# GLA half chunks laid between the MLA blocks, rotated keys on 128 rows, and softmax normalised by a diagonal matmul

## The chip, the cores and the metric

The kernel runs on one core of one Trainium2 chip. The metric is the time of one execution on the device in microseconds; several runs are compared by their median. TensorE is called PE, VectorE DVE, ScalarE ACT, GpSimd POOL, and SyncE SP; PEld is PE's loading of weights (the stationary operand). A matmul whose operands fill r partitions is said to use r rows of PE. PE's clock has two levels here, 1.2 GHz (a granted clock of 0.50) and 2.4 GHz (1.00).

## The reference, cut to what matters

The program is one inference step of a two-layer encoder on 272 prompt tokens (16 of them learned) and 32 sample tokens. Layer 0 starts with a mixer of two parallel parts, and only this stage is touched:

```python
# GLA, 4 heads (dk 64, dv 128), chunks of 64 tokens, state s of each head carried along
o_inter = einsum('bhtd,bhdv->bhtv', qc * exp(b), s)
att = einsum('bhtd,bhsd,bhtsd->bhts', qc, kc, decay)
o = o_inter + einsum('bhts,bhsv->bhtv', att, vc)
s = exp(b_last)[..., None] * s + einsum('bhsd,bhsv->bhdv', kc * exp(b_last - b), vc)
...
o_gla = rms_norm(o_gla, gla_norm_g) * silu(r)
# MLA, 8 heads over shared latent keys (128) and rotated keys (32)
s = (einsum('bhqc,bkc->bhqk', ql, k_lat) + einsum('bhqr,bkr->bhqk', qr, k_rope)) * MLA_SCALE
p = softmax(where(k_chunk <= q_chunk, s, NEG_INF))
o_lat = einsum('bhqk,bkc->bhqc', p, k_lat)
...
out = concatenate([o_gla, o_mla]) @ w_out0
```

The rest (layer norms, a routed MoE with 64 experts in each layer, a pooling mixer in layer 1) is the same in both kernels.

## The kernel before

All tokens lie in three tiles (`TILES`) of 128, 128 and 64 rows; the last holds 16 prompt tokens and the 32 sample tokens. There are six GLA chunks, `CHUNKS`: 0 to 3 are 64 tokens of the prompt, 4 its last 16, and 5 the sample, with a state of its own (`s_s`; the prompt's is `s_p`). All matrices are float32.

The order of the work on each engine is that of the code, written out by hand. PSUM is eight banks that `bank_uses` deals out in turn, by a list of named uses; use n of the list can't start before use n - 8 has been emptied (`banks.open`), `banks.full` waits for the fill and `banks.copied` for the emptying of a use. The uses of this stage, and who empties them:

- `att(t, h)`: level products of GLA, seven per chunk, K and M of 64 (L1005). DVE masks and sums them (`sum_levels`, L1621 and L1625) into `att`.
- `ql(h)`: absorbed queries, 64 rows, 320 columns (L1032); ACT copies them to `q_lat`. `qrT(i)`: `q_rot` transposed (24 transposes, L749); ACT copies them to `q_rot_t`.
- `o(c, j)` and `u(c, j)`, for each chunk c and pair of heads j: output of the chunk (L1018, the state against `qe_t` on 128 rows, and L1022, `att` against `v` on 64 rows or fewer) and update of the state (L1025). ACT copies `o` to `og`; `update_state` on DVE (L1637) adds `u` to the state, which the next chunk needs.
- `s(i)`, `pt(i)`, `ol(i)` for the 19 attention blocks: block 2h has head h's first 128 queries and 144 keys, block 2h + 1 the next 128 and 272 keys; block 16 packs the last prompt queries of all heads (272 keys), 17 and 18 the sample's (320 keys). `s` is two matmuls in one sum, `kv_t` on 128 rows and `kr_t` on 32. `scores` on DVE adds the mask and takes the maximum (L1670, L1672, L1493), ACT takes exp with its sum (L1375), DVE the reciprocal (L1684) and the product with it (L1493). PE transposes the probabilities (`pt`, L749: two tiles for 144 keys, three for 272 or 320, the last of 16 or 64 keys), ACT copies them to `p_t`, PE multiplies them with `ckv_n` or `past` (`ol`, L765, one matmul per key tile, the last on 16 or 64 rows), and DVE copies that back into `q_lat` (`latent_out`, L1497). A float32 matmul shows as two instructions in the trace, a transpose as one.

The block loop on PE issues for each i: s(i), pt(i - 2), ol(i - 3). DVE does for each m: reciprocal and product of m, `scores(m + 2)`, `latent_out(m - 2)`. All level products and chunks stand ahead of the loop, tile by tile. Between them and the blocks the squares of `og` are summed (`gss`), ACT makes `grs` of them with two changes of its table, and `norm_out` scales `og` after blocks 1, 3 and 5. After the loop come the transposes of `og` (`ogT`, waiting for `og_ready`), `om`, and the output projection `mo` (starts at 249.28 us). POOL sends the GLA states out when the last `u` is done, and SP waits for `og_ready` before it loads the router and the shared expert.

## Time and profile before

| | |
|---|---|
| median of 3 runs | 1508.03 us (1506.62 to 1508.96) |
| the profiled execution | 1507.37 us, span 1505.6 us |
| PE busy | 1435.9 us, 95% of the span |
| DVE, ACT, POOL busy | 634.3, 348.5, 49.1 us |
| mean granted clock of PE | 0.942 |
| this stage, level products to the start of `mo` | 102 to 249.3 us |

Busy time is what the engine's own instructions cover; where matmuls overlap or load weights in between, PE counts as busy all the time. The granted clock is the share of 2.4 GHz in a stretch; a stretch that spans a change shows a value between 0.50 and 1.00.

### The profile page before, as it was taken

Reading aid. Unit: us, or ns where it says so; the run is one execution under the profiler, and the core shown is the slowest. Engines: PE = TensorE matmul, PEld = TensorE weight load, DVE = VectorE, ACT = ScalarE, POOL = GpSimd, SP = SyncE. Lnnn points to the kernel's source line nnn. Section 1 sums busy time; section 2 is a strip of 40 time slices with the busy share of each in tenths; the row PEclk is TensorE's granted clock in tenths of the full one; section 3 lists DMA queues with packets and bytes.
Section 4 is the critical chain, followed back from the end, with each engine's and each line's share of the span. In section 5 each row is a group of like instructions: output and inputs, shape, how many; then the busy total and the mean of one; then the engine's idle time right before and its main releaser. Section 6 shows DMA issues by size and latency. Waiting matters only on the chain.

```text
span 1505.6 us, 17800 instructions
## 1 busy us (share of the span) xinstructions
PE 1435.9 (95%) x6519; PEld 753.0 (50%) x6519; DVE 634.3 (42%) x1267; ACT 348.5 (23%) x722; POOL 49.1 (3%) x77
## 2 busy tenths in 40 slices
PE   6999899899999999999999978999999999999994
PEld 4565465464454454455445465545445445444542
DVE  0554542562433343344334368334334333433436
ACT  1441321221221222122122213122212122222211
POOL 5200100100000000000000020000000000000000
PEclk9996557899999999999999989999999999999997
DMA  9102020176998999899899842599989989998970
GB/s 297 62 6 113 8 91 0 65 300 270 375 391 349 410 387 393 366 394 392 347 412 391 349 151 103 205 372 391 390 364 395 392 348 410 390 390 364 395 305 31
DMA packets 63623, 435.21 MB, mean 289 GB/s; under 512 B 4324, under 2 KB 6436, under 8 KB 13537
## 3 DMA queue, kind: packets, MB, share of 16 engines
q1 hardware_dynamic: 60800, 427.08, 71.0%
q0 software_dynamic: 2784, 7.62, 1.6%
q8 instruction: 24, 0.39, 0.1%
q14 instruction: 15, 0.12, 0.0%
HBM read 432.93 MB, written 1.76 MB: 289 GB/s over the span
## 4 chain that ended last, share of the span: by engine, by line
PE 93%; DVE 4%; issue 1%; ACT 1%; DMA 0%; SPq 0%; DVEq 0%
PE bank L849 30%; PE bank L765 25%; PE bank L797 15%; PE bank L791 12%; PE bank L749 4%; PE bank L859 1%; PE bank L919 1%; DVE sb_x L1519 1%; PE bank L1025 1%; PE bank L906 1%; DVE sb_x L1515 1%; PE bank L1022 1%; DVE sb_ln_st L1511 1%; PE bank L1018 1%; DMA sb_x<-in_x_sample_dram 0%
## 5 line engine op out<-in xcount | busy, mean ns | idle before, releaser
L1448 DVE TENSOR_TENSOR sb_x<-sb_x,bank 128x512 f32<-128x512 f32 (+1 forms) x396 | 242.0, 678 | 118.7 <-PE bank L791 118.7
L797 PE MATMUL bank<-sb_wslot,sb_ht 128*64 128x512 f32 x1024 | 231.0, 593 | 0.0
L849 PE MATMUL bank<-sb_wslot,sb_xg_own 128*64 128x512 f32 x1024 | 226.5, 595 | 1.7 <-ACT sb_xg_own L1216 1.7
L849 PE MATMUL bank<-sb_wslot,sb_xt 128*64 128x512 f32 x1024 | 226.8, 595 | 0.0
L1467 DVE TENSOR_TENSOR sb_hh<-sb_sg,bank 128x256 f32<-128x256 f32 x64 | 27.0, 421 | 376.8 <-ACT sb_sg L1240 376.8
L1454 DVE SCALAR_TENSOR_TENSOR sb_yl<-bank,sb_gslot,sb_yh 128x512 fp32r<-128x512 f32 x128 | 96.0, 750 | 162.8 <-ACT sb_yh L1222 162.8
L765 PE MATMUL bank<-sb_pick,sb_xh 128*128 128x512 f32 x432 | 160.8, 401 | 0.9 <-DVE sb_x L1817 0.9
L791 PE MATMUL bank<-sb_yh,sb_place 128*128 128x512 f32 x396 | 157.6, 398 | 3.3 <-DVE sb_yl L1454 3.3
L791 PE MATMUL bank<-sb_yl,sb_place 128*128 128x512 f32 x396 | 156.6, 395 | 0.0
L1240 ACT ACTIVATE sb_sg<-bank 128x256 f32<-128x256 f32 x64 | 24.6, 384 | 550.1 <-PE bank L849 550.1
L797 PEld LDWEIGHTS bank<-sb_wslot,sb_ht 128*64 128x64 f32 x1024 | 72.8, 137 | 144.6 <-issue 139.3
L849 PEld LDWEIGHTS bank<-sb_wslot,sb_xg_own 128*64 128x64 f32 x1024 | 71.4, 137 | 140.6 <-issue 139.6
L849 PEld LDWEIGHTS bank<-sb_wslot,sb_xt 128*64 128x64 f32 x1024 | 70.7, 137 | 139.5 <-issue 139.5
L1222 ACT ACTIVATE sb_yh<-bank,sb_gslot 128x512 fp32r<-128x512 f32 x128 | 88.1, 688 | 174.2 <-PE bank L797 174.2
L765 PE MATMUL bank<-sb_pick,sb_xl 128*128 128x512 f32 x288 | 113.7, 395 | 0.0
L765 PEld LDWEIGHTS bank<-sb_pick,sb_xh 128*128 128x128 f32 x432 | 81.3, 188 | 19.1 <-issue 2.6
L791 PEld LDWEIGHTS bank<-sb_yh,sb_place 128*128 128x128 f32 x396 | 74.3, 188 | 27.3 <-DVE sb_x L1448 5.7
L791 PEld LDWEIGHTS bank<-sb_yl,sb_place 128*128 128x128 f32 x396 | 74.5, 188 | 17.1
L1216 ACT ACTIVATE sb_xg_own<-bank 128x512 f32<-128x512 f32 x80 | 47.9, 598 | 79.1 <-PE bank L765 79.1
L765 PEld LDWEIGHTS bank<-sb_pick,sb_xl 128*128 128x128 f32 x288 | 54.3, 188 | 10.1
L1216 ACT ACTIVATE sb_xt<-bank 128x512 f32<-128x512 f32 x64 | 38.3, 599 | 37.7 <-PE bank L765 37.7
L749 PEld LDWEIGHTS bank<-sb_cst,sb_hh 128*128 128x128 f32 x128 | 20.7, 205 | 46.0 <-issue 45.4
(297 smaller groups left out, 1201.1 us busy)
## 6 DMA issues: line engine op xcount, KB each, us to landing
sb_wslot<-in_moe_w_gate_dram SPq DMA_DIRECT2D x64, 2048.0 KB, 8.4
sb_wslot<-in_moe_w_up_dram SPq DMA_DIRECT2D x64, 2048.0 KB, 13.1
sb_wslot<-in_moe_w_down_dram SPq DMA_DIRECT2D x64, 2048.0 KB, 15.3
sb_w_in_hi<-in_w_in_dram SPq DMA_DIRECT2D x2, 2048.0 KB, 24.2
sb_w_in_lo<-in_w_out_dram SPq DMA_DIRECT2D x1, 4096.0 KB, 13.5
sb_w_in_lo<-in_w_in_dram SPq DMA_DIRECT2D x2, 1024.0 KB, 10.3
sb_ln_g<-in_ln_g_dram POOLq DMA_DIRECT2D x4, 512.0 KB, 4.5
sb_ln_b<-in_ln_b_dram POOLq DMA_DIRECT2D x4, 512.0 KB, 6.0
```

Source lines behind the costliest of these rows:

```text
L749: return pe.transpose(dst, src, ident[0:n, 0:n])
L765: last = pe.matmul(dst, lhs, rhs, start=i == 0, stop=i == len(pairs) - 1)
L791: last = pe.matmul(banks.tile[order[f]][:, :], place[u][:, t * P:(t + 1) * P], part[:, c * 512:(c + 1) * 512], start=h == 0, stop=h == 1)
L797: last = pe.matmul(y_b[c][64 * e:64 * e + 64, :], ht[:, k, 64 * e:64 * e + 64], w_down[u][:, e, k * D + c * 512:k * D + (c + 1) * 512], st ...
L849: last = pe.matmul(gu_b[64 * e:64 * e + 64, :], xgt[b][:, k, sl], w_gu[u][:, :, e, k * FE:(k + 1) * FE], start=k == 0, stop=k == DK_SLICES ...
L859: last = pe.matmul(place_b[:, t * PLACED:(t + 1) * PLACED], pick[b][:, t, q * P:(q + 1) * P], spread[:, b, t, :], start=True, stop=True)
L1216: act.activation(xgt[b][:, kk, :], banks.tile[2 + c][:, :], ACT.Copy).then_inc(s[f"xg_copied{c}"], 1)
L1222: act.activation(yh[:, c * 512:(c + 1) * 512], banks.tile[4 + c][:, :], ACT.Copy, scale=gslot[:, u, :]).then_inc(s[f"yh_ready{c}"], 1)
L1240: act.activation(sg[:, :], gu_b[:, 0:FE], ACT.Silu).then_inc(s["sg_ready"], 1)
L1448: dve.tensor_tensor(dst, dst, banks.tile[order[f]][0:rows, :], ALU.add).then_inc(s["added"], 1)
L1454: dve.scalar_tensor_tensor(out=yl[:, cc], in0=banks.tile[4 + c][:, :], scalar=gslot[:, u, :], in1=yh[:, cc].bitcast(F32), op0=ALU.mult, op ...
L1467: dve.tensor_tensor(hh[:, :], sg[:, :], gu_b[:, FE:2 * FE], ALU.mult).then_inc(s["h_ready"], 1)
```

## The change

It has three parts.

1. `CHUNK_PARTS` splits the six chunks into twelve half chunks (c, j), and one of them stands behind each of the first twelve iterations of the block loop: on PE `chunk_out(c, j)`, on ACT the copy of `o`, on DVE `update_state(c, j)` behind `latent_out`. All level products, `ql` and `qrT` come ahead of the loop. The squares of a tile are summed behind iterations 6, 10 and 13 of DVE's loop, `grs` is made in iteration 15 of ACT's, and `norm_out` stands in iterations 16, 17 and 18.
2. `kr_t` and `skr_t` get 128 rows, of which 32 to 127 are zero (one more memset on POOL), and `kr_t`'s matmul in `s` runs on 128 rows.
3. DVE doesn't multiply the probabilities by the reciprocal any more. POOL multiplies the identity by it (`diag`, 128x128, two buffers, the second use waits for `pt(m - 2)`), and `pt` becomes a float32 matmul of the raw exponentials against `diag`, which transposes and normalises.

POOL's 19 `diag` instructions stand ahead of its stores of the GLA states.

```diff
+CHUNK_PARTS = [(c, j) for c in range(len(CHUNKS)) for j in range(2)]
+SQUARES_AT = (6, 10, 13)
+ROOT_AT, NORM_AT = 15, (16, 17, 18)
@@ bank_uses
-    for t in range(TILES):
-        u += [("att", t, h) for h in range(GH)]
...
+    u += [("att", t, h) for t in range(2) for h in range(GH)] + [("ql", h) for h in range(MH)]
+    u += [("att", 2, h) for h in range(GH)] + [("qrT", i) for i in range(5)]
     n = len(attention_blocks())
     for i in range(n + 3):
         u += [("s", i)] if i < n else []
         u += [("pt", i - 2)] if 0 <= i - 2 < n else []
         u += [("ol", i - 3)] if 0 <= i - 3 < n else []
+        u += [("o",) + CHUNK_PARTS[i], ("u",) + CHUNK_PARTS[i]] if i < len(CHUNK_PARTS) else []
@@ gpsimd
+            gp.memset(kr_t[:, :], 0.0).then_inc(zeroed, 1)
...
+            for m in range(len(attention_blocks())):
+                gp.wait_ge(inv_ready, m + 1)
+                if m >= 2:
+                    banks.full(gp, ("pt", m - 2))
+                gp.tensor_scalar(diag[:, m % 2, :], const("ident"), stat[:, m % 4, 3:4], None, ALU.mult).then_inc(diag_ready, 1)
@@ tensor engine
-                    ql, qr = q_lat[:, hs[0], q0:q0 + nq], q_rot_t[0:ROPE, hs[0], q0:q0 + nq]
+                    ql, qr = q_lat[:, hs[0], q0:q0 + nq], q_rot_t[:, hs[0], q0:q0 + nq]
...
-                    pe.wait_ge(p_ready, m + 1)
+                    pe.wait_ge(diag_ready, m + 1)
                     ps = banks.open(pe, ("pt", m))
                     for k, rows in key_tiles(m):
-                        last = transpose(pe, ps[0:rows, k * P:(k + 1) * P], sm[:, m % 4, k * P:k * P + rows])
+                        last = pe.matmul(ps[0:rows, k * P:(k + 1) * P], sm[:, m % 4, k * P:k * P + rows], diag[:, m % 2, :],
+                                         start=True, stop=True)
...
+                if i < len(CHUNK_PARTS):
+                    chunk_out(*CHUNK_PARTS[i])
@@ scalar engine, block loop
+                if m < len(CHUNK_PARTS):
+                    c, j = CHUNK_PARTS[m]
+                    tc, pb, n = CHUNKS[c]
+                    copy(og[pb:pb + n, tc, j * 256:(j + 1) * 256], ("o", c, j), lambda ps: ps[pb:pb + n, 0:256])
+                if m == ROOT_AT:
+                    act.wait_ge(gss_ready, TILES)
+                    rsqrt(grs[:, :], gss[:, :], 1.0 / GDV, eps[:, 1:2], grs_ready)
@@ vector engine, block loop
                 dve.wait_ge(ex_ready, m + 1)
-                step(dve.reciprocal(stat[:, m % 4, 3:4], stat[:, m % 4, 2:3]))
-                ts(sm[:, m % 4, 0:nk], sm[:, m % 4, 0:nk], stat[:, m % 4, 3:4], None, ALU.mult, None, p_ready)
+                dve.reciprocal(stat[:, m % 4, 3:4], stat[:, m % 4, 2:3]).then_inc(inv_ready, 1)
                 if m + 2 < len(blocks):
                     scores(m + 2)
                 if m >= 2:
                     latent_out(m - 2)
-                if m == 0:
+                if m < len(CHUNK_PARTS):
+                    update_state(*CHUNK_PARTS[m])
+                if m in SQUARES_AT:
+                    square_sums(SQUARES_AT.index(m))
+                if m == NORM_AT[0]:
                     dve.wait_ge(grs_ready, 1)
-                if m in (1, 3, 5):
-                    norm_out(m // 2)
+                if m in NORM_AT:
+                    norm_out(NORM_AT.index(m))
```

On PE, an odd slot of the block loop before: s with 272 keys, a pt of three tiles, an ol of two. `waits` names semaphores: emptied2 says that bank 2 is free, p_ready that the probabilities are normalised; `sb_w_in_hi` is the memory that `q_lat`, `q_rot_t`, `sm` and `p_t` share, and sizes are those of output rows and columns.

```order
L765 MATMUL bank0<-sb_kv_t,sb_w_in_hi 128x272 [waits emptied0]
L765 MATMUL bank0<-sb_kr_t,sb_w_in_hi 128x272
L749 MATMUL bank1<-sb_cst,sb_w_in_hi 128x128 [waits emptied1,p_ready]
L749 MATMUL bank1<-sb_cst,sb_w_in_hi 128x128
L749 MATMUL bank1<-sb_cst,sb_w_in_hi 16x128
L765 MATMUL bank2<-sb_w_in_hi,sb_ckv_n 128x128 [waits emptied2,emptied6]
L765 MATMUL bank2<-sb_w_in_hi,sb_ckv_n 128x128
```

The same slot (i = 5) now:

```order
L770 MATMUL bank4<-sb_kv_t,sb_w_in_hi 128x272 [waits emptied4]
L770 MATMUL bank4<-sb_kr_t,sb_w_in_hi 128x272
L1082 MATMUL bank5<-sb_diag,sb_w_in_hi 128x128 [waits emptied5,diag_ready]
L1082 MATMUL bank5<-sb_diag,sb_w_in_hi 128x128
L1082 MATMUL bank5<-sb_diag,sb_w_in_hi 16x128
L770 MATMUL bank6<-sb_w_in_hi,sb_ckv_n 128x128 [waits emptied6,emptied0]
L770 MATMUL bank6<-sb_w_in_hi,sb_ckv_n 128x128
L1021 MATMUL bank7<-sb_s_p,sb_qe_t 64x256 [waits emptied7,emptied6]
L1025 MATMUL bank7<-sb_v,sb_att 64x128 [waits att_ready] x2
L1028 MATMUL bank0<-sb_v,sb_kd 128x256 [waits emptied0]
```

Behind ol there now stand the output and the update of a half chunk. The bank of ol, bank 6, was that of the `u` of two slots before, and the chunk's first matmul waits for the same emptying (emptied6).

On DVE, one iteration of the block loop before, from a product of the probabilities on (`filled` says that PE has filled a bank):

```order
L1493 TENSOR_SCALAR sb_w_in_hi<-sb_w_in_hi,sb_stat 128x144 [waits dve_step]
L1670 SCALAR_TENSOR_TENSOR sb_w_in_hi<-bank5,sb_mix 128x144 [waits filled5,filled0,p_ready]
L1672 TENSOR_REDUCE sb_stat<-sb_w_in_hi 128x1 [waits emptied5]
L1493 TENSOR_SCALAR sb_stat<-sb_stat 128x1 [waits dve_step]
L1497 COPY sb_w_in_hi<-bank4 128x128 [waits filled4,mx_ready]
```

The iteration that belongs to the slot shown for PE, now:

```order
L1683 RECIPROCAL sb_stat<-sb_stat 128x1 [waits ex_ready,emptied1]
L1670 SCALAR_TENSOR_TENSOR sb_w_in_hi<-bank4,sb_mix 128x272 [waits filled4,filled3]
L1672 TENSOR_REDUCE sb_stat<-sb_w_in_hi 128x1 [waits emptied4]
L1496 TENSOR_SCALAR sb_stat<-sb_stat 128x1 [waits dve_step]
L1500 COPY sb_w_in_hi<-bank1 128x128 [waits filled1,mx_ready]
L1639 SCALAR_TENSOR_TENSOR sb_s_p<-sb_s_p,sb_u_t,bank6 64x128 [waits filled6]
L1639 SCALAR_TENSOR_TENSOR sb_s_p<-sb_s_p,sb_u_t,bank6 64x128 [waits dve_step]
```

The product is gone, and two instructions that add `u` of bank 6 to the state are now behind scores of bank 4 and the copy of bank 1.

## Rows read from the trace of the kernel before

**Rows 1.** The page, parts 1 and 2: busy time; granted clock in 40 slices.
```profile
PE 1435.9 (95%) x6519; PEld 753.0 (50%) x6519; DVE 634.3 (42%) x1267; ACT 348.5 (23%) x722; POOL 49.1 (3%) x77
...
PEclk9996557899999999999999989999999999999997
```

**Rows 2.** Windows: length, busy us (instructions) by engine, granted clock, DMA share, GB/s.
```profile
107.50:111.20 3.70, 2.20 (x7) 0.87 (x8) 3.09 (x4) 1.33 (x4) 0.00 (x0) 1.00 0.00 0
...
116.50:121.50 5.00, 5.00 (x113) 4.96 (x112) 3.72 (x6) 0.00 (x0) 0.00 (x0) 0.50 0.02 3
121.50:124.85 3.35, 3.35 (x20) 2.23 (x16) 3.15 (x5) 1.67 (x3) 0.00 (x0) 0.50 0.00 0
...
131.00:135.10 4.10, 2.40 (x11) 0.83 (x10) 3.71 (x12) 0.38 (x1) 0.00 (x0) 1.00 0.81 277
135.10:159.40 24.30, 20.95 (x52) 8.75 (x52) 6.10 (x18) 3.93 (x12) 0.00 (x0) 0.50 0.31 126
...
171.80:241.80 70.00, 70.00 (x200) 44.01 (x199) 29.82 (x103) 17.29 (x67) 0.00 (x0) 0.50 0.12 49
```

**Rows 3.** Timeline of PE, 121 to 250 us: start, us, instructions.
```profile
121.58 4.05 PE L749 MATMUL bank<-sb_cst,sb_q_rot 128*32 128x128 f32 x24
...
249.28 1.10 PE L765 MATMUL bank<-sb_w_in_lo,sb_xt 128*128 128x512 f32 x2 [0.94 <-DVE sb_xt L1497]
```

**Rows 4.** Timeline of PE, two slots of the attention blocks.
```profile
188.12 0.85 PE L765 MATMUL bank<-sb_kv_t,sb_w_in_hi 128*128 128x144 f32 x2
188.90 0.84 PE L765 MATMUL bank<-sb_kr_t,sb_w_in_hi 32*128 32x144 f32 x2
...
191.87 1.27 PE L765 MATMUL bank<-sb_kv_t,sb_w_in_hi 128*128 128x272 f32 x2
193.07 1.27 PE L765 MATMUL bank<-sb_kr_t,sb_w_in_hi 32*128 32x272 f32 x2
194.28 0.90 PE L749 MATMUL bank<-sb_cst,sb_w_in_hi 128*128 128x128 f32 x3
194.97 1.36 PE L765 MATMUL bank<-sb_w_in_hi,sb_ckv_n 128*128 128x128 f32 x4
196.26 0.61 PE L765 MATMUL bank<-sb_kv_t,sb_w_in_hi 128*128 128x144 f32 x1
```

**Rows 5.** Timeline of PE, half chunks at both clocks.
```profile
125.55 0.65 PE L1018 MATMUL bank<-sb_s_p,sb_qe_t 128*64 128x256 f32 x2
...
127.33 0.65 PE L1018 MATMUL bank<-sb_s_p,sb_qe_t 128*64 128x256 f32 x2
...
137.60 1.11 PE L1018 MATMUL bank<-sb_s_p,sb_qe_t 128*64 128x256 f32 x2
...
140.84 1.11 PE L1018 MATMUL bank<-sb_s_p,sb_qe_t 128*64 128x256 f32 x2
```

**Rows 6.** Timeline of DVE, state updates and two blocks.
```profile
137.78 0.73 DVE L1637 SCALAR_TENSOR_TENSOR sb_s_s<-sb_s_s,sb_u_t,bank 64x128 f32<-64x128 f32 x2 [1.18 <-PE bank L1025]
...
189.88 0.31 DVE L1670 SCALAR_TENSOR_TENSOR sb_w_in_hi<-bank,sb_mix 128x144 f32<-128x144 f32 x1 [0.28 <-PE bank L765]
...
190.75 0.29 DVE L1497 COPY sb_w_in_hi<-bank 128x128 f32<-128x128 f32 x1
...
194.48 0.44 DVE L1670 SCALAR_TENSOR_TENSOR sb_w_in_hi<-bank,sb_mix 128x272 f32<-128x272 f32 x1 [2.98 <-PE bank L765]
...
195.62 0.29 DVE L1497 COPY sb_w_in_hi<-bank 128x128 f32<-128x128 f32 x1
```

**Rows 7.** Groups of POOL: busy us, mean ns.
```profile
L720 POOL TENSOR_TENSOR sb_wslot<-sb_wslot 128x1024 f32<-128x1024 f32 x2 | 4.7, 2336 | 571.6 <-DMA sb_wslot<-in_pool_scale_dram 571.6
```

**Rows 8.** Timeline: level sums on DVE, a table load on ACT.
```profile
104.28 0.62 DVE L1621 TENSOR_TENSOR sb_att_m<-bank,sb_mix 128x448 f32<-128x448 f32 x1
...
105.89 0.62 DVE L1621 TENSOR_TENSOR sb_att_m<-bank,sb_mix 128x448 f32<-128x448 f32 x1
...
159.22 1.28 ACT L1269 ACT_TABLE_LOAD   x1
```

More of the change, by code:

```diff
@@ L62 @@
 SLOTS = 64
-ZEROED = 2 + 9 + 2
+ZEROED = 2 + 9 + 3
 MIX_PARAMS = 11
@@ L400, in build @@
         stat = mb("stat", [P, 4, 4])
+        diag = mb("diag", [P, 2, P])
         mixer_ctx.close()
@@ L1323, in _ @@
                 act.activation(kv_t[:, cols], ps[:, 256:256 + rows], ACT.Copy)
-                act.activation(kr_t[:, cols], ps[0:ROPE, 384:384 + rows], ACT.Copy).then_inc(banks.empty_sem(n), 1)
+                act.activation(kr_t[0:ROPE, cols], ps[0:ROPE, 384:384 + rows], ACT.Copy).then_inc(banks.empty_sem(n), 1)
             for g in range(TILES):
@@ L1626, in sum_levels, with update_state @@
                              att_ready if i + 1 == len(parts_) else None)
-            def update_state(c):
+            def update_state(c, j):
                 t, pb, n = CHUNKS[c]
                 st = s_s if c == 5 else s_p
-                for j in range(2):
-                    name = ("u", c, j)
-                    ps = banks.full(dve, name)
-                    last = t * P + pb + n - 1
-                    for b in range(2):
-                        hp, hc = slice(64 * b, 64 * b + 64), slice(128 * b, 128 * b + 128)
-                        ins = dve.scalar_tensor_tensor(out=st[hp, j, hc], in0=st[hp, j, hc], scalar=u_t[hp, j, last:last + 1],
-                                                       in1=ps[hp, hc], op0=ALU.mult, op1=ALU.add)
-                        step.banked(ins, banks, name) if b else step(ins)
+                name = ("u", c, j)
+                ps = banks.full(dve, name)
+                last = t * P + pb + n - 1
+                for b in range(2):
+                    hp, hc = slice(64 * b, 64 * b + 64), slice(128 * b, 128 * b + 128)
+                    ins = dve.scalar_tensor_tensor(out=st[hp, j, hc], in0=st[hp, j, hc], scalar=u_t[hp, j, last:last + 1],
+                                                   in1=ps[hp, hc], op0=ALU.mult, op1=ALU.add)
+                    step.banked(ins, banks, name) if b else step(ins)
             dve.wait_ge(state_in, 16 * GH)
@@ L1643, in _, with square_sums @@
                 sum_levels(t)
-                for c in CHUNKS_BY_TILE[t]:
-                    update_state(c)
-            for c in range(len(CHUNKS)):
-                for j in range(2):
+            def square_sums(t):
+                rows = ROWS[t]
+                for c, j in CHUNK_PARTS[4 * t:4 * t + 4]:
                     banks.copied(dve, ("o", c, j))
-            for t in range(TILES):
-                rows = ROWS[t]
                 tt(sq[0:rows, :], og[0:rows, t, :], og[0:rows, t, :], ALU.mult)
```

85 lines of the change are left out of this document (33 added, 52 removed).

## The prediction

> **What bounds the kernel now.** I read the page first. PE is busy 95% of the span [rows 1], so time can only come from shorter or faster work on PE or from its gaps. The change touches one stage, so next I cut that stage with the windows view [rows 2]. From the level products (102 us) to the output projection (249.3 us [rows 3]) PE runs at two speeds: the granted clock is 1.00 (2.4 GHz) to 111.2, 0.50 (1.2 GHz) to 124.85, 1.00 to 135.1, and 0.50 from there to about 248 (the clock row of the page has a 7 in its seventh slice, 225.8 to 263.5) [rows 1, 2]. PE is busy 70.00 of 70.00 us in the attention blocks and still has half its clock. Nothing waits for DVE there: DVE works 29.8 us and ACT 17.3 us of the 70. So the 112 us at 0.50 are the prize, and the number of PE cycles is the second item.
>
> What did PE do before the clock moved? [rows 2, 3] It rose at 124.85 after transposes of q_rot, all with 128 rows and without gaps, since 121.58 us. It did not rise after five full microseconds of level products on 64 rows (116.5 to 121.5), nor in 24 us of GLA chunks, nor in 70 us of blocks, where kr_t occupies 32 rows, the last key tile 16, and 128-row work comes in shorter pieces [rows 4]. It fell at 111.2 and 135.1 after stretches in which PE was busy 2.20 of 3.70 us and 2.40 of 4.10 us, with 64 rows and fewer. Rows used and gaps are what differs; I take that as the mechanism.
>
> The Trainium skill ("TensorE: Matmul & The Clock Gate", Part 4: PE-mode transpose) says that transposes do not bring the full clock, as they don't count as PE-busy in the same way. This trace disagrees: the rise at 124.85 follows transposes alone. By that rule matmuls in the place of the blocks' transposes would bring the full clock and the time of the case "full throughout" below.
>
> By the row, transposes are as good as any 128-row work for the clock, so I credit their replacement with nothing.
>
> **The change, part by part, in PE time at 0.50.** A *slot* is what PE does for one i of the block loop: s, pt, ol and, new, a half chunk. Before, an even slot (144 keys) takes 188.12 to 191.87 = 3.75 us and an odd one (272 keys) 191.87 to 196.25 = 4.38 [rows 4], 8.13 a pair.
> - *pt as matmul*: kv_t takes 0.78 us for 144 columns and 1.20 for 272, so 128 columns stream in 0.42 us. A transposed tile takes (194.97 - 194.28)/3 = 0.23 [rows 4]. Five tiles a pair: +5 x 0.2 = +1.0 us.
> - *kr on 128 rows*: kr_t costs as much as kv_t (0.78, 1.20), so more rows cost nothing. Of each 0.78, 144 x 0.42/128 = 0.47 streams and 0.31 does not; four matmuls of the ol tiles take 1.29 us from 194.97 for 0.85 of streaming, so part of this time goes where the number of rows stays the same. If kr and the first pt tile lose it: -0.3 to -0.5 a slot; nothing and -0.6 are the bounds. With the line above: 8.0 to 9.1 us a pair, and I take 8.2.
> - *Half chunks moved*: one takes 137.60 to 140.84 = 3.24 us at 0.50, and 125.55 to 127.33 = 1.78 at 1.00 [rows 5]. Twelve move, none vanishes. PE's idle time around them, 3.35 us of 135.1 to 159.4 alone [rows 2], goes.
> - *DVE*: 19 normalisations of the probabilities go, each shorter than a scores instruction of the same columns (0.31, 0.44) [rows 6]. POOL gets 19 tensor_scalar of 128x128. The trace has none; the nearest row is a two-input product of 128x1024 at 2.34 us, which is 0.29 for 128 columns and the other bound whole [rows 7]. I take 0.45, near the end with the same columns. It lies under s and pt of later slots as long as chunks stand between them; in the tail at the full clock each 0.5 us more would cost up to 4.
> - *kr_t memset*: one more at the start, where POOL waits for w_in next. The state stores now stand behind 19 diag instructions on POOL and the shared loads of SP behind a late og_ready; both are needed only after mo. Nothing.
>
> **The new wait.** This is what the order decides. DVE runs scores(i), latent_out(i-4), update_state(i-2) in that order, and scores(i) waits for s(i). On PE, ol(i-3) of slot i opens the bank that u(i-2) used (eight banks in turn, five uses a slot), and chunk i needs the state of i-2. So in slots 4 to 12 PE does s(i), pt(i-2), then stands until DVE is through: 0.2 us from the end of s to DVE (194.28 to 194.48), scores 1.14 (272 keys) or 0.87 (144), latent_out 0.33, two state updates 0.77 (0.29 and 0.73 and the steps between), 0.07 back [rows 4, 6]: 2.5 us in odd slots, 2.25 in even ones. Behind the standing ol(i-3) in PE's queue are the chunk and s(i+1), for which DVE waits in turn. pt covers 1.28 (three tiles) or 0.85 at 0.50, and half of that at 1.00.
>
> s at 0.50 is 1.20 + 1.21 - 0.3 = 2.1 us in odd slots and 0.78 + 0.78 - 0.3 = 1.25 in even ones; ol is 1.15 (the 1.29 above less what I count with the next s) and a tile more, 1.6.
>
> At 0.50: odd 2.1 (s) + 2.5 + 1.15 (ol) + 3.24 = 9.0; even 1.25 + 2.25 + 1.6 + 3.24 = 8.3. At 1.00: odd 1.07 + 2.5 + 0.58 + 1.78 = 5.95; even 0.63 + 2.25 + 0.79 + 1.78 = 5.45. Slots 0 to 3 have less to wait for, no wait in the first two and no latent_out in the next: 4.5 + 5.3 + 6.4 + 7.8 = 24.0 us at 0.50, 2.4 + 2.9 + 4.3 + 5.0 = 14.6 at 1.00. Slots 4 to 11: 8 x 8.65 = 69.2, or 8 x 5.7 = 45.6. So the chunk slots are 93.2 or 60.2 us.
>
> *Start.* DVE's level sums (104.28 to 105.89, 1.61 us a head [rows 8]) pace the absorbed queries, which reuse their banks: 104.28 + 8 x 1.61 = 117.2, then one ql, tile 2's levels (an estimate of 3.7 for both at 0.50), the rotations (4.05 [rows 3]), and ACT's last copies (an estimate of 1.6): slot 0 at 126.7.
>
> *Tail* (slots 12 to 21): 40.4 us of PE at 0.50 (four slots of 4.1 with 1.8 of the wait, then the 320-key blocks and the drain, 22 us now). At 1.00: 20.2 plus about 6.3 of waits, since reciprocals now queue behind square_sums and norm_out (an estimate of 1.4 us each) and exp behind grs with two table loads of 1.3 each [rows 8]: 26.5. From the last ol to mo: 241.8 to 249.28, 7.5 at 0.50 [rows 2, 3], 4.9 at 1.00.
>
> *Sums against the 249.28 at which mo starts in the profiled execution:*
> - clock full throughout: 126.7 + 60.2 + 26.5 + 4.9 = 218.3, or -31.
> - half in the chunk slots, full again early in the tail, where no chunk stands between runs of 128 rows (about 8 us at 0.50 first, then 32.4/2 and 5.3 of the waits, 29.5): 126.7 + 93.2 + 29.5 + 4.9 = 254, or +4 to +5.
> - half throughout: 126.7 + 93.2 + 40.4 + 7.5 = 267.8, or +18.5.
>
> With a share h of the chunk slots at 0.50 it is about -30 + 33h. The profiled execution is 1507.37 (span 1505.6) and the median 1508.03, 0.7 apart, so differences carry over.
>
> **Which h?** An odd slot at 0.50 now has s and pt unbroken on 128 rows, 2.1 + 1.3 = 3.4 us, like the 3.3 us of transposes after which the clock rose, but only once in 17 us, with a wait behind it. Each slot at 1.00 has 1.85 us of standing still, then a 16-row tile and 64-row products, much like what stood before both falls. So I expect it to rise at the rotations or in the first blocks, to fall again once or twice, and to be full in the tail. I choose h = 0.6: -9 to -10 us, **1499 us**. By case: h under 0.2 (1477 to 1485), 0.28; mixed (1485 to 1506), 0.42.
>
> **Rivals.**
> - *All full* (case one, 0.28): 1477, if a standing PE of 1.85 us a slot is too little to lower the clock. For: before both falls PE stood for 1.5 and 1.7 us and the rest had 64 rows and fewer, while here s, pt and half of the chunk have 128. Against: the 1.85 us in every slot.
> - *Half in the chunk slots* (0.20): 1508 to 1513. For: the chunks, which at 0.50 never raised the clock in 24 us, are laid between the runs of 128 rows. It decides from h = 0.9 up.
> - *Half throughout* (0.10): slower, +18.5, 1526. One mechanism: the ping-pong of PE and DVE adds about 1.3 us to eight slots and the tail's waits cut its runs too. It speaks against it that plain slots have over 3.4 us without a break.
> - *Transposes hold the clock down* (0.05, within the first case): as matmuls they would let s, pt and ol run as one piece that raises and keeps the clock, and the time is that of all full, 1477. Against: the row of the q_rot transposes ahead of the rise at 124.85.
> - *The wait isn't there* (within the first case): then chunk slots at 0.50 are 7.3 us and at 1.00 3.7; 1461 at full clock. Against: the order of DVE.
>
> **Chances.** A measurement tells about 0.2%, 3 us, from no change. Faster 0.68, same 0.12 (half of the third case and the edge of the mixed one), slower 0.20. The range reaches from all full to the third case: 1476 to 1514; the likeliest case's own is 1485 to 1506. The time left out is half throughout and the absent wait.
>
> **What would show it.** Right: slot 0 near 127; chunk slots of 5.5 or 8.7 us; PE waiting for update_state before ol or qe in each, 1.8 us at 1.00 and 1.3 at 0.50; no PE wait for diag in slots 2 to 11; clock changes inside the stage; time after mo unchanged. Wrong: the clock 0.50 to the end of the tail; diag instructions over 1 us with pt waiting for them; pairs of plain slots over 8.5 us at 0.50, if unhidden weight loads remain between kr and pt.

## The result and the profile after

The changed kernel takes 1515.3 us (median of 20 executions) against 1507.7 for the kernel before (20 beside them): a ratio of 1.0047, 95% interval 1.0037 to 1.0058. It is slower by 7 to 8 us; the forecast was 9 us faster. The profiled execution has a span of 1511.8 us, 6.2 more than before, and the output projection starts 6.15 us later (255.43 against 249.28 [rows 3]), so all of it lies ahead of the projection. Of all executions below, two stand far out and enter no ratio: one of e9_tail_only took 2085.7 us at a mean clock of 0.644, one of the kernel before 4939 us.

The page of the changed kernel, busy time and granted clock, against [rows 1]:

```profile
PE 1432.3 (95%) x6568; PEld 755.0 (50%) x6568; DVE 627.9 (42%) x1248; ACT 349.1 (23%) x723; POOL 61.5 (4%) x97
...
PEclk9996558999999999999999988999999999999997
```

The slices moved a little: 5 5 8 9 where 5 5 7 8 9 stood. So I cut the changed kernel's stage at the places where the clock moves (windows view; columns as in [rows 2]):

```profile
120.96:124.37 3.41, 1.47 (x16) 1.02 (x14) 2.45 (x8) 3.27 (x9) 0.00 (x0) 1.00 0.97 386
124.37:144.85 20.48, 19.31 (x52) 11.11 (x52) 5.20 (x18) 4.06 (x13) 1.21 (x2) 0.50 0.33 135
144.85:151.68 6.83, 5.32 (x29) 3.18 (x29) 2.09 (x9) 2.34 (x10) 1.21 (x2) 1.00 0.00 0
151.68:175.57 23.89, 21.26 (x61) 12.92 (x60) 5.66 (x20) 2.96 (x13) 1.21 (x2) 0.50 0.00 1
175.57:182.40 6.83, 5.00 (x27) 3.28 (x28) 3.19 (x10) 2.13 (x8) 0.60 (x1) 1.00 0.00 0
182.40:189.22 6.82, 6.51 (x18) 3.33 (x18) 1.83 (x7) 0.27 (x1) 0.60 (x1) 0.50 0.00 0
189.22:192.64 3.42, 2.79 (x14) 1.58 (x15) 0.61 (x3) 1.03 (x5) 0.60 (x1) 1.00 0.01 2
192.64:223.36 30.72, 27.61 (x85) 17.51 (x84) 10.31 (x35) 5.55 (x23) 3.02 (x5) 0.50 0.00 1
223.36:240.42 17.06, 12.98 (x67) 8.90 (x66) 10.13 (x28) 7.42 (x20) 3.45 (x5) 1.00 0.00 0
240.42:254.08 13.66, 13.66 (x51) 9.26 (x52) 5.11 (x11) 2.56 (x6) 4.32 (x9) 0.50 0.71 268
```

The clock now rises four times in the blocks, and each time it is lost again. In each stretch at 1.00 PE is idle for part of the time (busy 5.32 of 6.83, 5.00 of 6.83, 2.79 of 3.42, 12.98 of 17.06). The waits view of PE, 124 to 256 us (us in total, times, longest), names what it stands for:

```profile
PE bank L770 <- DVE sb_s_p L1639: 8.9, 8, 1.5
PE bank L1082 <- POOL sb_diag L711: 4.1, 2, 2.6
...
PE bank L770 <- DVE sb_s_s L1639: 1.1, 1, 1.1
PE bank L1021 <- DVE sb_s_p L1639: 1.0, 1, 1.0
```

L1639 is update_state, 11.0 us in ten waits; L711 is GpSimd's diagonal. PE's timeline, an even slot begun at 1.00 and the odd one after it at 0.50:

```profile
147.20 0.51 PE L770 MATMUL bank<-sb_kv_t,sb_w_in_hi 128*128 128x144 f32 x2
147.55 0.41 PE L770 MATMUL bank<-sb_kr_t,sb_w_in_hi 128*128 128x144 f32 x2
147.79 0.71 PE L1082 MATMUL bank<-sb_diag,sb_w_in_hi 128*128 128x128 f32 x4
150.01 1.10 PE L770 MATMUL bank<-sb_w_in_hi,sb_ckv_n 128*128 128x128 f32 x6 [1.51 <-DVE sb_s_p L1639]
...
153.78 1.27 PE L770 MATMUL bank<-sb_kv_t,sb_w_in_hi 128*128 128x272 f32 x2
...
155.75 1.60 PE L1082 MATMUL bank<-sb_diag,sb_w_in_hi 128*128 128x128 f32 x6
158.28 1.49 PE L770 MATMUL bank<-sb_w_in_hi,sb_ckv_n 128*128 128x128 f32 x4 [0.93 <-DVE sb_s_p L1639]
...
239.41 1.07 PE L1082 MATMUL bank<-sb_diag,sb_w_in_hi 128*128 128x128 f32 x6 [2.65 <-POOL sb_diag L711]
240.41 1.94 PE L770 MATMUL bank<-sb_w_in_hi,sb_ckv_n 128*128 128x128 f32 x6
```

The wait is where the prediction put it and a little shorter than it said (1.51 for 1.8 at 1.00, 0.93 to 1.09 for 1.2 to 1.4 at 0.50). Two of the three falls in the chunk slots, at 151.68 and 182.40, come 1.7 and 1.1 us after such a wait. But the slots at 0.50 have the wait too, and two of the rises (175.57 and 189.22) fell inside one, so this trace alone does not show that the wait lowers the clock; the experiments ask that. The last two rows are the tail: PE stands 2.65 us for the diagonal of block 17, and 1 us later the clock falls and stays down for 13.66 us. DVE's timeline shows why that diagonal is late:

```profile
236.49 0.68 DVE L1493 TENSOR_TENSOR sb_og<-sb_og,sb_grs 128x512 f32<-128x512 f32 x1
237.20 0.69 DVE L1493 TENSOR_TENSOR sb_og<-sb_og,sb_g_gla 128x512 f32<-128x512 f32 x1
237.93 0.16 DVE L1683 RECIPROCAL sb_stat<-sb_stat 128x1 f32<-128x1 f32 x1
```

The reciprocal stands behind a whole norm_out, which stands behind the scores of block 18. The diagonal then took 1.17 us (from 238.19) beside the next norm_out, where the other 18 took 0.60 or 0.61 us. The groups of POOL give the price of a diagonal, the unknown of the prediction (busy us, mean ns):

```profile
L711 POOL TENSOR_SCALAR sb_diag<-sb_cst,sb_stat 128x128 f32<-128x128 f32 x19 | 12.1, 634 | 151.8 <-DVE sb_stat L1683 151.8
```

**The balance.** The same cut of the kernel before, windows view:

```profile
111.19:124.85 13.66, 13.66 (x142) 9.77 (x142) 7.56 (x12) 2.42 (x5) 0.00 (x0) 0.50 0.01 1
124.85:135.09 10.24, 8.54 (x126) 4.51 (x124) 5.94 (x19) 2.36 (x6) 0.00 (x0) 1.00 0.33 112
135.09:247.73 112.64, 107.09 (x301) 62.16 (x303) 48.39 (x149) 26.95 (x93) 4.20 (x8) 0.50 0.15 60
```

From 111 us to the projection, count PE's busy time at 0.50 once and at 1.00 twice: that is its work in microseconds at 0.50. Before, 120.8 us busy at 0.50 and 9.2 at 1.00 (0.6 of them after 247.73) make 139.1, and PE is idle 8.2 of 138.1 us. Now 98.1 (9.7 of them before 120.96) and 28.0 make 154.1, and it is idle 18.6 of 144.7. So work grew by 15.0 and idle time by 10.4, and 18.8 more busy microseconds at the full clock gave back 18.8: +6.6, by which this stretch is longer. Three questions follow: what lifts the clock, what lowers it, and which part made PE's work 15 us more.

### The profile page after: what moved, and what is told of

Its sections match the earlier page's. It is cut to its first block, busy times and chain, and to the rows that moved or that the text cites. A ratio compares the mean times of both kernels' runs of the same rounds, so it can differ in the third digit from the quotient of the medians.

```text
span 1511.8 us, 17919 instructions
## 1 busy us (share of the span) xinstructions
PE 1432.3 (95%) x6568; PEld 755.0 (50%) x6568; DVE 627.9 (42%) x1248; ACT 349.1 (23%) x723; POOL 61.5 (4%) x97
## 4 chain that ended last, share of the span: by engine, by line
PE 91%; DVE 5%; issue 2%; ACT 1%; DMA 1%; SPq 0%; POOL 0%; DVEq 0%; ACTq 0%; POOLq 0%
PE bank L854 30%; PE bank L770 24%; PE bank L802 15%; PE bank L796 12%; PE bank L754 3%; PE bank L864 1%; PE bank L924 1%; PE bank L1028 1%; PE bank L1025 1%; PE bank L911 1%; PE bank L1021 1%; DVE sb_x L1522 1%; DVE sb_ln_st L1514 1%; DVE sb_x L1518 1%; DMA sb_x<-in_x_sample_dram 1%
```

## Experiments

The changed kernel has three parts: half chunks between the blocks (part 1), the rotated keys and queries on 128 rows (part 2), and transposing by a matmul with the diagonal (part 3). Each run below was timed 5 to 12 times beside the kernel before; ratios are to that, with the 95% interval. The theories that the expectations name are: A, rows used and gaps set the clock; T, transposes hold it down; S, the keys on 32 rows hold it down; I, laying chunks between blocks lifts it; W, a standing PE lowers it; R, the 64-row and 16-row products lower it whatever PE waits for.

**Which part lifts the clock?** The first two runs split part 1 from the other two: `e1_parts_2_3` is the kernel before with parts 2 and 3, `e2_part_1` the changed kernel without them.

```diff
 # e1_parts_2_3, against the kernel before
-        kr_t = mb("kr_t", [ROPE, T_COLS])
+        kr_t = mb("kr_t", [P, T_COLS])
...
-                        last = transpose(pe, ps[0:rows, k * P:(k + 1) * P], sm[:, m % 4, k * P:k * P + rows])
+                        last = pe.matmul(ps[0:rows, k * P:(k + 1) * P], sm[:, m % 4, k * P:k * P + rows], diag[:, m % 2, :],
+                                         start=True, stop=True)
 # e2_part_1, against the changed kernel: both of these the other way round
```

> The kernel before with the diagonal and the keys on 128 rows, but the chunks where they stood: all six ahead of the blocks. The blocks follow one another with nothing of 64 rows between them, only the 16-row key tiles. Theory A (rows and gaps set the clock; transposes are as good as other 128-row work): a pair of blocks at 0.50 costs about what it did (8.1 us before, 8.2 by my sum), and since s, pt and ol had the same share of full rows before, the clock stays at 0.50 for most of the stage: -3 to +3 us against before. Rival T (transposes held the clock down; the Trainium skill, TensorE: Matmul & The Clock Gate, Part 4, says that they do not count as the matmuls do): with them gone the clock rises in the first blocks and the 86 us of blocks at 0.50 become about 50: -30 us or more. Rival S (the rotated keys on 32 rows held it down) gives the same time; the trace alone does not part S from T here, kernels with one of the two do.

Measured: 1489.8 us, 0.9879 (0.9859 to 0.9899), -18 us. Theory A as I had it (-3 to +3) falls, as it gave the wider keys no weight in the blocks; which of T and S it is, e5 and e6 below say. The clock was at 1.00 in two stretches of the blocks, of 10.24 us and this one (windows view):

```profile
190.20:220.92 30.72, 29.88 (x158) 21.35 (x158) 13.77 (x53) 10.61 (x42) 8.34 (x15) 1.00 0.22 88
```

> The changed kernel with the half chunks between the blocks, but transposes, normalisation on DVE and 32-row keys as before. Theory A (rows and gaps): at least as slow as the changed kernel, since the slots hold less 128-row work and DVE has 0.8 us more to do per slot ahead of update_state: the granted clock at 0.50 in nearly all of 126 to 250 and +10 to +20 us against before. Rival T (transposes are what keeps the clock down, in the changed kernel it was lifted where they went): no rise at all in the chunk slots and the tail, and +18 or more. Rival I (interleaving is what lifted the clock, whatever the tiles are): rises as in the changed kernel, five of them between 120 and 250, and 0 to +8 us.

Measured: 1526.8 us, 1.0126 (1.0105 to 1.0146), +19. Part 1 alone never lifts the clock: rival I falls, and A and T both foresaw this. The windows view of this run, one row from the rotations to the end of the stage:

```profile
123.90:263.80 139.90, 123.64 (x327) 67.20 (x327) 48.11 (x151) 28.54 (x96) 4.20 (x8) 0.50 0.08 31
```

**Rows or transposes?** Parts 2 and 3 were then taken singly on the kernel before.

```diff
 # e5_kr_only, against the kernel before: part 2 alone
-                        ql, qr = q_lat[:, hs[0], q0:q0 + nq], q_rot_t[0:ROPE, hs[0], q0:q0 + nq]
+                        ql, qr = q_lat[:, hs[0], q0:q0 + nq], q_rot_t[:, hs[0], q0:q0 + nq]
 # e6_diag_only, against the kernel before: part 3 alone
-                    pe.wait_ge(p_ready, m + 1)
+                    pe.wait_ge(diag_ready, m + 1)
```

> The kernel before with the rotated keys and queries on 128 rows and nothing else; transposes, DVE's normalisation and the place of the chunks stay. The run with both edits and the old place of the chunks took 1489.8 against 1507.8 and its clock was at 1.00 in 40.9 of the 73 us from 158 to 231, so one of the two (or both together) lifts it. Rival T (the transposes held it down): the clock stays at 0.50 to the end of the blocks, and only the weight loads between kr and pt go, -3 to -7 us. Rival S (the 32 rows held it down): the clock rises in the blocks, -20 to -30 us. If both edits are needed: as T.

Measured: 1481.0 us, 0.9836 (0.9821 to 0.9851), -26. One edit, and a better kernel than the change.

> The kernel before with the transposes replaced by matmuls with the diagonal from GpSimd, and nothing else; the rotated keys stay on 32 rows. Rival T: the clock rises in the blocks, -10 to -20 us. Rival S: it stays at 0.50, each tile costs 0.2 us more, 45 tiles or about +9 us, and the first slots wait for the diagonal as they did in the run with both (7.0 us in all there): +5 to +12 us. If both edits are needed: as S.

Measured: 1528.5 us, 1.0143 (1.0122 to 1.0165), +22. The windows of e5, then of e6:

```profile
186.91:222.17 35.26, 31.15 (x181) 22.79 (x181) 24.93 (x83) 14.34 (x52) 0.00 (x0) 1.00 0.24 98
```

```profile
134.20:267.30 133.10, 127.64 (x350) 72.17 (x352) 41.48 (x129) 26.46 (x93) 15.61 (x27) 0.50 0.13 50
```

With transposes and 128-row keys the clock rises for good 27 us into the blocks and stays at 1.00 to the projection; with matmuls for transposes and 32-row keys it never moves. Rival T falls, and rival S stands. What about the 32 rows does it is not shown: the same edit also takes 0.36 us a slot off PE (below), so these runs do not part the number of rows from whatever PE does in that time around a 32-row matmul.

The Trainium skill's rule that transposes do not bring the full clock ("TensorE: Matmul & The Clock Gate", Part 4) would have it the other way round; these two runs disagree with it.

e6 also prices part 3. PE's timeline of e6, an odd slot and an even one, against [rows 4]:

```profile
198.14 1.27 PE L772 MATMUL bank<-sb_kv_t,sb_w_in_hi 128*128 128x272 f32 x2
199.35 1.27 PE L772 MATMUL bank<-sb_kr_t,sb_w_in_hi 32*128 32x272 f32 x2
200.55 1.76 PE L1087 MATMUL bank<-sb_diag,sb_w_in_hi 128*128 128x128 f32 x6
202.24 1.52 PE L772 MATMUL bank<-sb_w_in_hi,sb_ckv_n 128*128 128x128 f32 x4
...
208.38 1.27 PE L772 MATMUL bank<-sb_kv_t,sb_w_in_hi 128*128 128x272 f32 x2
```

A pair takes 208.38 - 198.14 = 10.24 us where it took 8.13: +2.1, not the +1.0 of the sum. Three tiles take 1.69 us (200.55 to 202.24) where three transposes took 0.69 (194.28 to 194.97), and two products of the ol tiles behind them 1.45 for 1.29. Part 2 alone takes a pair from 8.13 to 7.42 (175.27 to 183.11 in e5, less a wait of 0.42). The changed kernel, with both, has 4.14 + 4.95 = 9.1 (slots 12 and 13, less a wait of 1.09). For 9.5 pairs, 0.95 us each, that is 9 of the 15 us by which the balance's work grew; the rest I have not traced.

**Do PE's waits lower the clock?** Two versions of the changed kernel keep all three parts and move only DVE's work.

```diff
 # e3_update_first, against the changed kernel
                 dve.reciprocal(stat[:, m % 4, 3:4], stat[:, m % 4, 2:3]).then_inc(inv_ready, 1)
+                if m < len(CHUNK_PARTS):
+                    update_state(*CHUNK_PARTS[m])
                 if m + 2 < len(blocks):
                     scores(m + 2)
                 if m >= 2:
                     latent_out(m - 2)
-                if m < len(CHUNK_PARTS):
-                    update_state(*CHUNK_PARTS[m])
 # e4_dve_ahead, on top of that: no scores(1) ahead of the loop; SQUARES_AT = (6, 10, 12), ROOT_AT = 13,
 # NORM_AT = (15, 16, 17); square_sums and norm_out here too, and then
-                if m + 2 < len(blocks):
-                    scores(m + 2)
-                if m >= 2:
-                    latent_out(m - 2)
+                if m + 1 < len(blocks):
+                    scores(m + 1)
+                if m >= 3:
+                    latent_out(m - 3)
```

> The changed kernel with one line moved: DVE does update_state(i) ahead of scores(i+2), not behind it. This takes away the wait of PE's ol for DVE (10 times, 1.0 to 1.5 us each, 11.0 us in all). Theory W (the standing PE is what lowers the clock in the chunk slots): the clock is at 1.00 for most of slots 0 to 11, they last 12 x 4 = 48 us instead of 85, so the kernel takes about 1480. Rival R (the 64-row products and 16-row tiles lower it, wait or not): the clock changes as often as before, only the waits go, slots of 7.3 us at 0.50 and 4 at 1.00, 8 to 12 us less than the changed kernel, about 1504.

Measured: 1477.1 us, 0.9801 (0.9779 to 0.9824): 38 us less than the changed kernel for one statement moved, of which 11 are the waits themselves. Its windows and one slot of its timeline:

```profile
122.91:136.56 13.65, 13.21 (x35) 7.16 (x36) 4.07 (x15) 3.93 (x12) 1.21 (x2) 0.50 0.54 217
136.56:201.41 64.85, 60.28 (x314) 39.29 (x314) 33.68 (x111) 23.03 (x81) 11.13 (x18) 1.00 0.00 1
201.41:211.66 10.25, 10.25 (x41) 7.31 (x41) 3.88 (x8) 2.23 (x6) 3.87 (x8) 0.50 0.69 254
```

```profile
142.18 0.51 PE L770 MATMUL bank<-sb_kv_t,sb_w_in_hi 128*128 128x144 f32 x2
...
146.24 0.72 PE L770 MATMUL bank<-sb_kv_t,sb_w_in_hi 128*128 128x272 f32 x2
```

Slots of 4.1 us, no wait in them, and the clock at 1.00 for 64.85 us: theory W holds here and rival R falls, since the 64-row products and the 16-row tiles are all still there. The clock falls once, after the 2.65 us for the diagonal of block 17, as in the changed kernel; a wait of 1.07 us for a diagonal at 188.4, at 1.00, is followed by no fall.

> The changed kernel with DVE's loop laid out anew: reciprocal, update_state, square_sums or norm_out, and only then the scores of the next block (one block ahead instead of two), so that the reciprocals, and with them the diagonals, are never queued behind a scores instruction that waits for PE; rsqrt on ACT comes two blocks earlier. This takes away the waits for update_state (11.0 us) and those for the diagonal (1.44 and 2.65 us, after which the clock fell at 240.4). Theory W: the clock stays at 1.00 from the first slots to the output projection, chunk slots 48 us, tail 22: about 1470. Rival R: it changes as often as in the changed kernel; chunk slots as in the run with update_state alone moved, and the tail's waits of 4 us go: 1500 to 1503.

Measured: 1471.4 us, 0.9766 (0.9743 to 0.9789). Two waits of about 1 us remain for the last diagonals, and the fall at 200.6 comes between them, so the full clock to the projection, which theory W had, did not come.

**The waits gone and the rows given back.** e8_first_kr32 is e3 with the keys on 32 rows, e7_first_transposes e3 with transposes.

```diff
 # e7_first_transposes, against e3_update_first
-                dve.reciprocal(stat[:, m % 4, 3:4], stat[:, m % 4, 2:3]).then_inc(inv_ready, 1)
+                step(dve.reciprocal(stat[:, m % 4, 3:4], stat[:, m % 4, 2:3]))
+                ts(sm[:, m % 4, 0:nk], sm[:, m % 4, 0:nk], stat[:, m % 4, 3:4], None, ALU.mult, None, p_ready)
 # e8_first_kr32, against e3_update_first
-        kr_t = mb("kr_t", [P, T_COLS])
+        kr_t = mb("kr_t", [ROPE, T_COLS])
 ... (skr_t, q_few_rot and the rows of qr likewise)
```

> The same run (1477.1 us) with the rotated keys and queries back on 32 rows; diagonal and half chunks between the blocks stay. If the 32 rows count (rival S): clock at 0.50 for most of 123 to 240, 1500 to 1510. If they do not (T or W): clock at 1.00 as there, and only the weight loads between kr and pt come back, 0.15 to 0.25 us a slot at the full clock: 1480 to 1483.

Measured: 1527.7 us, 1.0156 (1.0133 to 1.0179), 51 us more than e3, more than either theory said. Its windows view:

```profile
124.75:268.05 143.30, 142.96 (x388) 78.75 (x390) 42.15 (x135) 27.58 (x95) 15.62 (x27) 0.50 0.10 38
```

PE is busy 142.96 of 143.30 us, with matmuls where transposes stood, and the clock does not rise once. A PE that hardly ever stands is not enough; with the keys on 32 rows the clock stays down.

> The run with update_state ahead of the scores (1477.1 us, clock at 1.00 from 136.6 to 201.4), but with the transposes and DVE's normalisation back; half chunks between the blocks and keys on 128 rows stay. Rival T: without matmuls in the place of the transposes the clock falls back to 0.50 for all of 123 to 240 and the run takes 1500 to 1515. Rival W (the waits alone made the difference between the changed kernel and that run): the clock is at 1.00 as there, and the cheaper tiles make it 1470 to 1478.

Measured: three executions took 1463 to 1471 us and three 1496 to 1499 (median of all 1483.4; mean clocks 0.968 to 0.975 and 0.945 to 0.948). The ratio of 0.9738 (0.971 to 0.9766) is that of the first kind alone. Neither theory said two kinds. The profiled execution is of the first, at 1.00 from 139.1 to 180.1 us.

**The tail alone.**

```diff
 # e9_tail_only, against the changed kernel
-SQUARES_AT = (6, 10, 13)
-ROOT_AT, NORM_AT = 15, (16, 17, 18)
+SQUARES_AT = (6, 10, 12)
+ROOT_AT, NORM_AT = 13, (16, 17, 18)
 # and from turn 12 on square_sums and norm_out stand between the reciprocal and scores(m + 2)
```

> The changed kernel (1515.3 us) with its tail alone laid out anew: the last square_sums and the norm_outs stand between the reciprocal and the scores, where DVE waits for PE, rsqrt comes two blocks earlier on ACT, and the last norm_out follows the last reciprocal. The wait for update_state in the chunk slots stays. Theory W as I have it: the standing of 1.44 and 2.65 us for the diagonal shrinks to 1 us each at most, the fall at 240.4 goes with it, and blocks, ogT and om run to their end at 1.00: -4 (a third of it waits, the rest 8 us of work at the full clock in place of half) to -8 us against the changed kernel, 1507 to 1511. Rival: the fall comes from what stands ahead of it, not from the length of these two waits: -1.5 to -3 us, 1512 to 1514.

Measured: 1506.8 us, 0.9986 (0.9974 to 0.9998) to the kernel before: 9 us less than the changed kernel. PE's timeline there has 0.90 us in the place of the 2.65:

```profile
239.32 1.07 PE L1082 MATMUL bank<-sb_diag,sb_w_in_hi 128*128 128x128 f32 x6 [0.90 <-POOL sb_diag L711]
...
242.38 2.18 PE L770 MATMUL bank<-sb_w_in_hi,sb_past 128*128 128x128 f32 x12
...
249.25 1.10 PE L770 MATMUL bank<-sb_w_in_lo,sb_xt 128*128 128x512 f32 x2 [0.96 <-DVE sb_xt L1500]
```

From slot 13 to the projection it takes 249.25 - 219.16 = 30.1 us, where the changed kernel took 255.43 - 214.72 = 40.7, and the clock stays at 1.00 from 222.94 on. Of these 10.6 us the profiled execution gives back 4.4, as it reaches slot 13 later, though nothing ahead of it was edited. The tail alone turns the change from slower into no difference.

**The best of it.** Part 2 and the moved DVE work stay, part 3 goes. e10_kr_ahead has the chunks ahead of the blocks, e11_ahead_transposes between them; e12_ahead_few also takes the four copies of the few queries out of the way of the first block.

```diff
 # e10_kr_ahead: e5_kr_only with DVE's loop as in e4; e11_ahead_transposes: e4 with the transposes of e7
 # e12_ahead_few, against e11 (PE)
-            pe.wait_ge(skeys_ready, 2)
+            pe.wait_ge(skeys_ready, 1)
...
+                    if i == 2 * MH:
+                        pe.wait_ge(skeys_ready, 2)
 # and on ACT the copies to q_few and q_few_rot stand in turn 0 of its loop
```

> The run with the keys on 128 rows alone (1481.0 us; chunks ahead of the blocks, transposes, normalisation on DVE), with DVE's loop one block ahead: reciprocal, normalisation and norm_out, then the scores. There PE waited for normalised probabilities 8 times, 7.7 us in all, the longest 3.9. If these waits keep the clock down in the first blocks (it rose for good at 186.9 only, 27 us into them), it rises 10 to 20 us earlier: 1468 to 1474. If not, only the waits after the first go: 1476 to 1479.

Measured: 1479.5 us, 0.9802 (0.9788 to 0.9816), 1.5 us less than e5 (5 by the two ratios). DVE's waits did not keep the clock down there. The windows view shows it at 0.50 for 27 us with PE busy for 26 of them, all on 128 rows but for the 16-row tiles, and then at 1.00 with the same work; why there and not before stays open.

```profile
168.81:196.12 27.31, 26.11 (x82) 19.38 (x82) 18.48 (x57) 8.64 (x35) 0.00 (x0) 0.50 0.32 126
196.12:217.00 20.88, 19.95 (x115) 15.62 (x114) 15.85 (x54) 9.23 (x39) 0.00 (x0) 1.00 0.00 1
```

> The run with DVE's loop one block ahead (1471.4 us: half chunks between the blocks, keys on 128 rows), with the transposes and DVE's normalisation in the place of GpSimd's diagonal. A pair of blocks at 0.50 took 10.24 us with matmuls and 8.13 with transposes, so about 1 us a pair at the full clock: -8 us, and DVE, with 0.5 us more a block, has room (it waits for PE 26.8 of 75 us): 1461 to 1465. Rival T in its last form (transposes make the clock less steady): 1475 to 1495 and a wide spread, as in the run of the update alone with transposes, which took 1463 to 1499.

Measured: again two kinds, 1458 to 1467 us (four) and 1492 to 1494 (four); the ratio of the first kind is 0.969 (0.9668 to 0.9713). The profiled execution is of the second kind, and PE is busy throughout in it at half its clock:

```profile
127.00:196.44 69.44, 69.44 (x197) 41.66 (x197) 27.27 (x87) 13.45 (x50) 0.00 (x0) 0.50 0.07 26
```

> The run with the loop one block ahead and transposes, with the four copies of the few queries on ACT moved from ahead of the first block into its first turn, and PE's wait for them ahead of the block that reads them. This takes away most of the 2.1 us in which PE stands ahead of the first block. Theory W: the clock then stays at 1.00 from the rotations on (it rose at 122.1 and fell at 125.5 just there), and the first three slots, 13 us at 0.50, take 7: -8 us against that run. Rival R (the level products on 64 rows ahead lower it whatever PE waits for): -1.5 to -2 us, the wait alone.

Measured: 1460.4 us, 0.9681 (0.9665 to 0.9696), all five of one kind (1458.8 to 1466.7). The fall at the first block is gone, with a wait of 0.98 us there instead of 2.1; windows and PE's timeline:

```profile
124.67:182.70 58.03, 53.52 (x282) 34.66 (x281) 39.77 (x127) 26.09 (x86) 4.21 (x8) 1.00 0.18 69
```

```profile
181.33 1.12 PE L763 MATMUL bank<-sb_w_in_hi,sb_ckv_n 128*128 128x128 f32 x6 [2.59 <-ACT sb_w_in_hi L1384]
...
194.23 0.90 PE L747 MATMUL bank<-sb_cst,sb_w_in_hi 128*128 128x128 f32 x3 [2.57 <-DVE sb_w_in_hi L1491]
```

The clock falls 1.4 us after the first wait of 2.6 us (182.70) and during the second (192.94).

**Two questions left by these.** Do transposes count for less, which would explain the two kinds? e13_twice does each of e11's twice. Do the falls in e12's tail go with its waits? e14_few_tail moves rsqrt and norm_out.

```diff
 # e13_twice, against e11_ahead_transposes
-                        last = transpose(pe, ps[0:rows, k * P:(k + 1) * P], sm[:, m % 4, k * P:k * P + rows])
+                        for again in range(2):
+                            last = transpose(pe, ps[0:rows, k * P:(k + 1) * P], sm[:, m % 4, k * P:k * P + rows])
 # e14_few_tail, against e12_ahead_few (and rsqrt behind the copies of pt, not ahead)
-ROOT_AT, NORM_AT = 13, (15, 16, 17)
+ROOT_AT, NORM_AT = 12, (14, 15, 18)
```

> The run with the loop one block ahead and transposes (11 above: its clock stayed at 0.50 through the chunk slots in 4 of 8 executions, 1492 to 1494 us, and rose early in the others, 1458 to 1467), with every transpose of the probabilities done twice into the same place. The second ones do nothing but occupy 128 rows: a slot at 0.50 then has 3.9 us on 128 rows instead of 3.4, about what the matmuls with the diagonal gave, beside the same 3.3 us of chunk. Rival T (transposes count less for the clock than matmuls): at least as many executions stay at 0.50 as without, since the same matmuls are now thinner spread. Theory A (only the share of full rows in a slot counts): fewer or none stay at 0.50, as with the diagonal (0 of 10). In either case 5 tiles a pair more, +0.6 us a pair at 1.00: the executions that rise take 1463 to 1472.

Measured: 1470.8 us, 0.9748 (0.9722 to 0.9773), 1465.8 to 1474.8, none of five of the slower kind. Against 7 of 14 in e7 and e11, without the second transposes, this speaks against rival T: more transposes did not hold the clock down. It does not show that a transpose counts as much as a matmul, since e3 and e4, with matmuls, had none of ten of the slower kind. It is no proof, as five of one kind would come by chance 1 time in 32, and the clock of the profiled execution rose at 139.0, after the doubled transposes of one slot only.

> The fastest version so far (1460.4 us) with its tail changed: rsqrt on ACT behind the copies of the probabilities of block 12 and not ahead of those of block 13, and norm_out in turns 14, 15 and 18 instead of 15, 16 and 17. There PE stood 2.59 us for ACT and 1.47 and 2.57 us for DVE, and the clock fell right after the first and the last of them (182.7, 192.9). Theory W: with no standing over 1.5 us the clock stays at 1.00 to the output projection, 5 us of waits and 5 of clock go: 1450 to 1455. If the falls come whatever the waits do: 1456 to 1458.

Measured: 1459.6 us, 0.9676 (0.9658 to 0.9694), as e12. Its longest wait is 1.63 us, and the clock still fell twice:

```profile
176.26 0.44 PE L747 MATMUL bank<-sb_cst,sb_w_in_hi 128*128 128x128 f32 x2 [1.63 <-DVE sb_w_in_hi L1491]
```

```profile
178.22:185.04 6.82, 6.04 (x18) 3.57 (x17) 5.66 (x16) 1.96 (x8) 0.00 (x0) 0.50 0.00 0
```

The falls come 2.0 us after the wait of 1.63 us and during one of 1.13 (at 188.46). Either such waits are enough for a fall here, or the falls have another cause. Waits of this length do not always bring one: at 1.00 the changed kernel stood 1.44 us before 228.93, e3 1.07 and e5 1.01, and the clock stayed. Theory W's number for this run (1450 to 1455) was wrong, the other's (1456 to 1458) nearer, and what lowers the clock in the tail stays open. The two fastest versions are 48 us (3.2%) faster than the kernel before and 55 faster than the change.

## Why the prediction was wrong

- **The place and length of the new wait: right.** 1.51 us at 1.00 (said 1.8) and 0.93 to 1.09 at 0.50 (said 1.2 to 1.4). An odd slot at 0.50 took 9.15 us (153.78 to 162.93; said 9.0), an even one 8.46 (162.93 to 171.39; said 8.3). There was no wait for the diagonal in slots 2 to 11. A diagonal took 0.60 us and once 1.17, with pt waiting; 0.45 was in the sum, and over 1 us was named as a sign of being wrong.
- **Slot 0: near**, 124.54 for 126.7 (the terms given add up to 126.5).
- **What the sum missed by.** For 1499 us the projection had to start near 239.8: slot 0 at 126.7, 80.0 us of chunk slots (h = 0.6) and 33.1 from slot 12 on. It started at 255.43: slot 0 came 2.2 us early, the chunk slots took 5.0 us more and the tail 12.8 more.
- **h: too low, one of the two terms that failed.** I chose 0.6. The chunk slots took 124.54 to 209.49 = 85.0 us, which by -30 + 33h is h = 0.75, and 5 us more than chosen. The working said that a standing PE in every slot speaks against the full clock, and then gave more weight to the cases where it rises than to that. e3 shows that this wait is what kept it down: the same instructions without it ran at 1.00 for 65 us, and all five executions of e3 took 1474 to 1480.
- **The tail at the full clock: wrong, and the larger term.** The sum had 29.5 + 4.9 = 34.4 us from slot 12 to the projection even where the chunk slots ran at 0.50; it took 255.43 - 209.49 = 45.9, 11.5 more. About 9 of these are the clock: PE was busy 26.4 us at 0.50 there, where the sum had 8. The expected clock, "full in the tail", failed at both ends: it rose 13.9 us into the tail and not after 8, and it fell behind the wait for the diagonal of block 17. That wait was in the sum, for its length (about 6.3 us for all waits of the tail; 1.09 + 1.44 + 2.65 = 5.2 came). What was not in it is that the full clock can be lost behind a wait: 13.66 us of unbroken work followed at 0.50, half of it lost. e9, which shortens the wait to 0.90 us, has no fall there and takes 9 us less than the change. That it is the length of the wait is likely from e9 but not shown in general, as e14 has falls with shorter ones.
- **The matmul with the diagonal: mis-sized.** +1.0 us a pair of blocks in the sum, +2.1 in e6. The sum had 0.42 us for a tile against 0.23, which makes 1.26 for three; they took 1.69, and where the other 0.43 go no run shows. In the changed kernel a pair costs 9.1 us, the upper bound of the sum, not the 8.2 that I took; over 8.5 was named as a sign of being wrong.
- **Keys on 128 rows: right as a price, missed as a cause.** -0.36 us a slot, said -0.3 to -0.5. I had written that rows and gaps are what differs, and then asked only how the new slots would do, never what this edit would do alone in the blocks where PE never stood. Alone it was worth 26 us (e5), more than all I forecast for the change.
- **The rivals.** "Half in the chunk slots" (0.20) came nearest, but its +4 to +5 (+3 by the formula at h = 1) assumed a full tail; what came is a mixed case with a bad tail. "The wait isn't there" was priced at 1461; made so, e3 and e4 took 1477 and 1471, since tiles cost more and the first slots and the drain stay at 0.50. "Transposes hold the clock down" (0.05) fell with e5, e6 and e8. "Half throughout" was priced at 1526; e2 and e8, at 0.50 throughout, took 1527 and 1528, but they are other kernels, so that match is luck.
